# Another order of the gated products: v as a recursive product, gate b as an ordinary one, branch b joined by an adding DMA

## What is computed

```
xn = RMSNorm(x);  u, v, q, k, v_att, g_a, g_b = split(xn @ w_in);  u, v = gelu(u), gelu(v)
a  = u * (tril(W_s[g]) @ RMSNorm(v) + bias)          # chunks of 128 positions, 8 groups
b  = sliding-window attention(q, k, v_att)           # window 128, sinks, distance penalty
h  = sigmoid(g_a) * (a @ w_oa) + sigmoid(g_b) * (b @ w_ob)
x  = x + h @ w_out
x  = x + relu(RMSNorm(x) @ w_up)^2 @ w_down;  y = RMSNorm(x)
```

## Time and profile before

| | us |
|---|---|
| median of 3 runs | 1648.48 |
| lowest and highest | 1646.39, 1648.78 |
| the profiled execution | 1646.17 |
| its span in the trace | 1644.4 |
| mean granted TensorE clock in it | 0.975 of full |

### The profile page before, as it was taken

How to read it: one execution, slowest core, us unless ns; L and a number is a source line. 1 busy time by engine, 2 the same in 40 slices (tenths; PEclk the granted TensorE clock), 3 DMA queues, 4 the chain that set the end, 5 groups by cost and what they waited for, 6 DMA issues and landing times.

```text
span 1644.4 us, 28816 instructions
## 1 busy us (share of the span) xinstructions
PE 1558.3 (95%) x12226; PEld 1522.2 (93%) x12226; DVE 1063.0 (65%) x1385; ACT 764.7 (47%) x1158; POOL 171.1 (10%) x198
## 2 busy tenths in 40 slices
PE   3999999999998999989995999999999999999998
PEld 3988888889997999989995999999999999999997
DVE  3455554402656687666775776786787668767875
ACT  5465555522643555545441474533553355335533
POOL 4222322200001000000000040000000000000001
PEclk7899999999998999999997999999999999999999
DMA  7610110132974465665547444636363636454522
GB/s 243 194 28 25 31 29 21 34 90 78 230 255 133 103 167 155 193 180 162 134 141 233 127 104 103 164 94 179 81 177 92 165 105 153 115 142 127 131 64 104
DMA packets 108649, 209.09 MB, mean 127 GB/s; under 512 B 16816, under 2 KB 44464, under 8 KB 101192
## 3 DMA queue, kind: packets, MB, share of 16 engines
q1 hardware_dynamic: 93760, 140.32, 25.4%
q0 software_dynamic: 8208, 59.77, 18.5%
q10 hardware_dynamic: 6552, 7.13, 1.3%
HBM read 125.99 MB, written 23.53 MB: 91 GB/s over the span
## 4 chain that ended last, share of the span: by engine, by line
PE 80%; DMA 6%; DVE 5%; ACT 4%; issue 2%; SPq 1%; POOL 1%; DVEq 0%; ACTq 0%; POOLq 0%
PE ps L1537 63%; PE ps L1330 10%; PE ps L1318 2%; DMA og<-o_keep 1%; ACT prob L746 1%; DMA og<-h_keep 1%; PE ps L1376 1%; DVE prob L1008 1%; PE ps L1394 1%; DMA raw<-in_w_in 1%; POOL prob L580 1%; PE ps L1515 1%; DMA xn<-xn_keep 1%; SPq L407 1%; DVE y_t L1307 1%
## 5 line engine op out<-in xcount | busy, mean ns | idle before, releaser
L1537 PE MATMUL ps<-xp_hi,wp_hi 128*128 128x258 f32 x3136 | 635.6, 284 | 26.7 <-DVE xp_lo L1118 18.0
L1537 PE MATMUL ps<-xp_lo,wp_hi 128*128 128x258 f32 x3136 | 636.4, 284 | 0.0
L1537 PE MATMUL ps<-xp_hi,wp_lo 128*128 128x258 f32 x3136 | 635.2, 284 | 0.0
L1537 PEld LDWEIGHTS ps<-xp_hi,wp_hi 128*128 128x128 f32 x3136 | 491.1, 191 | 28.3 <-DVE xp_lo L1118 18.5
L1537 PEld LDWEIGHTS ps<-xp_hi,wp_lo 128*128 128x128 f32 x3136 | 490.7, 191 | 0.0
L1537 PEld LDWEIGHTS ps<-xp_lo,wp_hi 128*128 128x128 f32 x3136 | 487.6, 190 | 0.0
L682 ACT ACTIVATE wp_hi<-wbuf 128x1024 fp32r<-128x1024 f32 x196 | 208.0, 1061 | 569.3 <-PE ps L1537 563.7
L1112 DVE TENSOR_TENSOR wp_lo<-wbuf,wp_hi 128x1024 fp32r<-128x1024 f32 x196 | 243.5, 1242 | 163.7 <-ACT wp_hi L682 163.6
L1330 PE MATMUL ps<-xn_hi,w_hi 128*128 128x344 f32 x480 | 160.5, 334 | 2.5 <-DVE q_st L988 2.5
L1330 PE MATMUL ps<-xn_hi,w_lo 128*128 128x344 f32 x480 | 155.9, 325 | 0.0
L1330 PE MATMUL ps<-xn_lo,w_hi 128*128 128x344 f32 x480 | 155.9, 325 | 0.0
(11 more groups left out here) (188 smaller groups left out, 1559.8 us busy)
## 6 DMA issues: line engine op xcount, KB each, us to landing
wbuf<-wbuf POOLq DMA_DIRECT2D x57, 1024.0 KB, 7.6
wbuf<-in_w_up SPq DMA_DIRECT2D x24, 1024.0 KB, 5.5
wbuf<-in_w_down SPq DMA_DIRECT2D x24, 1024.0 KB, 5.1
wbuf<-in_w_in SPq DMA_DIRECT2D x18, 1024.0 KB, 6.6
raw<-in_w_in SPq DMA_DIRECT2D x40, 256.0 KB, 3.4
wbuf<-in_w_ob SPq DMA_DIRECT2D x6, 1024.0 KB, 8.6
wbuf<-in_w_oa SPq DMA_DIRECT2D x6, 1024.0 KB, 5.0
wbuf<-in_w_out SPq DMA_DIRECT2D x6, 1024.0 KB, 5.5
```

The lines of the kernel that those rows point to most:

```text
L1537: last = mm(ps[:, 2 * p + b, 0:HN], w[:, (2 * n + p // 2) % 2, k, p % 2 * P:(p % 2 + 1) * P], x[n % 2][:, k, b * HN:(b + 1) * HN], start=( ...
```

## The change

The order of groups becomes w_ob, v, u, gate a, w_oa, w_out: v is now group 1 (`G_V`), computed in seven block products with gelu on ACT half by half, and the v stage stands between `G_V` and `G_U`. The eight ordinary jobs of stage 1 now compute g_b; ACT copies it to `gate_b` (the place of `mix`) and takes the sigmoid at w = 0 to 7 of group 0. `finish_ob` on DVE multiplies each half of b @ w_ob by its half of `gate_b` and SP stores it to `h_keep`, once. In group G_OA, `finish_oa` only multiplies by gate a; the half of `h_keep` is added by a DMA that POOL issues (`add_h`). `og` and `o_keep` are gone. `xn` is reloaded in four quarters, from w = 12 of group 0 on, with no v stage behind it, and the load of s2 comes ahead of the results' stores at w = 12 (and ahead of `res` in G_OA). `gv_row` and `bb` are loaded at w = 10 of G_V. The first weight quarters of w_ob are loaded in another order and earlier, the buffers swap places, and `sgu_raw` moves.

```diff
-        G_OB, G_U, G_GB, G_GA, G_OA, G_OUT, G_UP = range(7)
+        G_OB, G_V, G_U, G_GA, G_OA, G_OUT, G_UP = range(7)
-        late = [G_OB, G_U, G_OUT, G_UP] + down
-        by_act = [G_U, G_GB, G_GA, G_OUT] + up
-        by_dve = [G_U, G_GB, G_OA] + up
+        late = [G_OB, G_V, G_U, G_OUT, G_UP] + down
+        by_act = [G_V, G_U, G_GA, G_OUT] + up
+        by_dve = [G_OB, G_U, G_OA] + up
...
-            def load_og(g, m):
-                src = o_keep if g == G_GB else h_keep
-                sp.dma_start(og[:, :, :], keep_half(src, m)).then_inc(og_in, 16)
...
+            sp.wait_ge(pv_done, NU)
+            load_quarter(0, "12")
             sp.wait_ge(db_ready, 1)
-            load_quarter(0, "12")
+            load_quarter(0, "11")
             sp.wait_ge(w_split, JW + 2)
             load_quarter(0, "s2")
-            sp.wait_ge(wt_turned, 1)
+            sp.wait_ge(job_done, JW + 1)
             load_quarter(0, "21")
-            sp.wait_ge(job_done, JW + 1)
-            load_quarter(0, "11")
             load_quarter(0, "22")
             for g in range(NM):
                 for w in range(14):
...
+                    if g == G_OB and w == 12:
+                        sp.wait_ge(xp_split, 2 * 7)
+                        for kh, th in ((1, 0), (0, 0), (0, 1), (1, 1)):
+                            cols = slice(th * HT, (th + 1) * HT)
+                            sp.dma_start(xn[:, MH * kh:MH * kh + MH, cols],
+                                         xn_keep[MH * P * kh:MH * P * (kh + 1), cols].rearrange("(k p) t -> p k t", p=P)).then_inc(xn_in[kh, th], 16)
+                    if w == 12 and g + 1 < NM:
+                        sp.wait_ge(wp_split, 14 * (g + 1))
+                        load_quarter(g + 1, "s2")
                     for e, m in finished(g, w):
-                        keep_and_fetch(e, m)
...
+                        if e == G_OB:
+                            sp.wait_ge(*dve_done(e, m))
+                            sp.dma_start(keep_half(h_keep, m), c_half(gate, m)).then_inc(h_kept[m // 2], 16)
...
+            def add_h(m):
+                pool.wait_ge(h_kept[m // 2], 2 * 16)
+                pool.wait_ge(*dve_done(G_OA, m))
+                pool.dma_start(c_half(h_t, m), keep_half(h_keep, m), accum_op=ALU.add).then_inc(h_added[m], 16)
...
-            add_s3(1)
+            add_s3(G_V)
+            add_s2(G_V)
+            add_s4(G_V)
+            add_s1(G_V)
+            add_s3(G_U)
             for t in range(NTOK):
...
                 add_s1(g)
+                if g == G_OA:
+                    for m in range(4):
+                        add_h(m)
+                    add_s3(G_OUT)
+                    for m in range(4, 8):
+                        add_h(m)
...
-                    elif g == G_U:
-                        act.wait_ge(xn_in[int(i != 1)], 16)
+                    elif g == G_V:
+                        act.wait_ge(xn_in[int(i != 1), int(i == 6)], 16)
...
                     elif g == G_OUT:
-                        act.wait_ge(*dve_done(G_OA, m))
+                        act.wait_ge(h_added[m], 16)
...
-                if g == G_OB and w == 13:
+                if g == G_V and w == 13:
                     for t in range(NTOK):
                         r, bank = ROWS[t], 2 * (t % 2)
+                        if t == 2:
+                            finish(G_V, 7)
...
+            def finish_ob(m):
+
+                mh, n = C_ORDER[m // 2][0], m % 2
+                dve.wait_ge(*c_moved(G_OB, m))
+                dve.wait_ge(gate_ready, MH * mh + 2 * n + 2)
                 c = c_half(gate, m)
-                tt(c, c, og[:, :, :], ALU.mult).then_inc(fin_v, 1)
+                tt(c, c, c_half(gate_b, m), ALU.mult).then_inc(fin_v, 1)
...
-                chain.link(tt(c, c, c_half(gate, m), ALU.mult))
-                dve.wait_ge(og_in, 16 * (8 + m + 1))
-                tt(c, c, og[:, :, :], ALU.add).then_inc(fin_v, 1)
+                tt(c, c, c_half(gate, m), ALU.mult).then_inc(fin_v, 1)
...
+                elif g == G_V:
+                    dve.wait_ge(xn_in[0, 0], 16)
+                    dve.wait_ge(xn_in[0, 1], 16)
...
                 elif g == G_OUT:
-                    dve.wait_ge(*dve_done(G_OA, 6 + n))
+                    dve.wait_ge(h_added[6 + n], 16)
...
             def turn_v(t):
                 r, bank = ROWS[t], 2 * (t % 2)
-                pe.wait_ge(*(moved(G_OB, 6, t) if t < 2 else (vn_ready, t - 1)))
+                pe.wait_ge(*act_done(G_V, 3 if t < 4 else 7))
+                pe.wait_ge(*(moved(G_V, 6, t) if t < 2 else (vn_ready, t - 1)))
```

More of the change, by code:

```diff
@@ L36, in build_trunk @@
                 sinks, w_oa, w_ob, w_out, ln2_g, w_up, w_down, lnf_g,
-                y_prompt, y_sample, k_win_p, v_win_p, k_win_s, v_win_s, sgu_v_s, x_keep, xn_keep, o_keep, h_keep):
+                y_prompt, y_sample, k_win_p, v_win_p, k_win_s, v_win_s, sgu_v_s, x_keep, xn_keep, h_keep):
     P = 128
@@ L144, in build_trunk @@
         xg = place("xg", [P, 3, KT, P], F32, r_2 + 4 * D)
+        gate_b = place("gate_b", [P, KT, T], F32, r_2)
         mix = place("mix", [P, KT, T], F32, r_2)
@@ L292, in build_trunk @@
         adds_up = [G_OUT] + down
[L293 to L295 removed]
+        late = [G_OB, G_V, G_U, G_OUT, G_UP] + down
+        by_act = [G_V, G_U, G_GA, G_OUT] + up
+        by_dve = [G_OB, G_U, G_OA] + up
         x_of = [b_all, xn, xn, xn, mix, h_t] + [xf, r_f] * NC
[L297 to L298 removed]
+        c_of = [gate, mix, gate, gate, h_t, res] + [r_f, res] * NC
+        w_of = [(w_ob, 0, 0), (w_in, 0, OV), (w_in, 0, OU), (w_in, 0, OGA), (w_oa, 0, 0), (w_out, 0, 0)]
         for c in range(NC):
@@ L497, in _ @@
                         load_quarter(g + 1, "22")
-                    if g == G_OB and w == 10:
-                        sp.wait_ge(xp_split, 2 * 6)
+                    if g == G_V and w == 10:
+                        sp.wait_ge(xp_split, 2 * (7 * G_V + 6))
                         sp.dma_start(gv_row[:, :], sgu_norm_g.to_broadcast([P, D])).then_inc(gain_in, 16)
@@ L652, in _ @@
                                         ALU.pow).then_inc(v_rstd, 1)
-            for g in range(1, NM):
-                if g not in (G_U, G_UP):
+            for g in range(G_U, NM):
+                if g not in (G_U, G_OUT, G_UP):
                     add_s3(g)
@@ L862, in out_act @@
                     m = 2 * C_ORDER.index(OUT_AT[i]) + p // 2
-                    if g == G_U and i == 0:
-                        act.wait_ge(o_kept, 8 * 16)
-                    elif g == G_GB:
+                    if g == G_V:
+                        act.wait_ge(*dve_done(G_OB, m))
+                    elif g == G_U:
+                        act.wait_ge(h_kept[m // 2], 2 * 16)
+                    elif g == G_GA:
                         act.wait_ge(*dve_done(G_U, m))
-                    elif g == G_GA:
-                        act.wait_ge(h_kept[m // 2], 2 * 16)
                     act.wait_ge(prod_done, 28 * g + 4 * i + p + 1)
@@ L877, in finish @@
                     nc.scalar.activation(c, c, ACT.Square).then_inc(fin_a, 1)
-                elif g in (G_U, G_GB, G_GA):
+                elif g in (G_V, G_U, G_GA):
                     act.wait_ge(*c_moved(g, m))
-                    nc.scalar.activation(c, c, ACT.Gelu_apprx_tanh if g == G_U else ACT.Sigmoid).then_inc(fin_a, 1)
+                    nc.scalar.activation(c, c, ACT.Sigmoid if g == G_GA else ACT.Gelu_apprx_tanh).then_inc(fin_a, 1)
                 elif g == G_OUT:
@@ L923, in _ @@
                 for e, m in finished(g, w):
-                    finish(e, m)
+                    if (e, m) != (G_V, 7):
+                        finish(e, m)
                 if g == G_OB and w < KT:
@@ L1187, in x_sum2 @@
                 b = blocks(g, n)
-                if g == G_U:
+                if g == G_V:
+                    dve.wait_ge(xn_in[1, 1], 16)
+                elif g == G_U:
                     dve.wait_ge(vs_stored, 16)
                     dve.wait_ge(mixed, NTOK)
-                    dve.wait_ge(xn_in[1], 16)
                 dve.wait_ge(t_added, t_count(g, 1 + n))
@@ L1271, in _ @@
                         finish_oa(m)
+                    elif e == G_OB:
+                        finish_ob(m)
                 if g == G_OB and w >= 12:
@@ L1288, in _ @@
                     variances(6).then_inc(var_ready, 1)
-                if (g, w) == (G_OB, 13):
+                if (g, w) == (G_V, 13):
                     out_dve(h)
@@ L1511, in mix_v @@
                 pe.wait_ge(vn_ready, t + 1)
-                pe.wait_ge(*(moved(G_OB, 6, 2 + t) if t < 2 else (mix_ready, t - 1)))
+                pe.wait_ge(*(moved(G_V, 6, 2 + t) if t < 2 else (mix_ready, t - 1)))
                 for g in range(GS):
@@ L1560, in _ @@
                     product(n // 7, n % 7, p)
-                    if n == 6 and p == 2:
-                        pe.wait_ge(v_ready, KT)
+                    if n == 7 * G_V + 6 and p == 2:
                         turn_v(0)
```

(4 more changed lines are left out.)

60 lines of the change are left out of this document (14 added, 46 removed).

## The result

The changed kernel took 1637.49 us as the median of 4 runs (1636.33 to 1638.29) beside 1648.18 of the kernel before (1646.39 to 1648.78): a ratio of 0.9945, interval 0.9923 to 0.9966. It is faster, by 10.7 us between the medians and by 9.1 (5.6 to 12.7) by the ratio, which is not the plain ratio of the two medians (0.9935). The forecast was 1629, in a range of 1615 to 1639: the direction and the range held, the size did not; 19.5 us of gain were forecast, and 8.8 of them (10.4 by the ratio) did not come. The profiled execution took 1637.21 us, its span 1635.5.

A forecast was written before the change was run, and what follows sets the result against it. PE, busy 1558.3 of 1644.4 us, was taken as the bound, with gain only from its stops or slow stretches. 1646.2 - 9.9 - 19.8 - 2.5 + 5.3 + 9.1 = 1628.4, plus 0.6: forecast 1629, range 1615 to 1639.

The forecast's parts named there:

- What goes: Stage 2: both waits for `og` and their stops are removed, 9.9 us and 19.8 us with the restarts.
- The v stage: Between G_V and G_U: shorter first stop and less slowed mixing, -2.5 us, bounds 0 and -3.5.
- First place, G_OB to G_V: PE waits before G_V behind the first quarter of `xn`, starting near T+3.3: +5.3 us with restart, at most +9.
- T: The end of G_OB, 494.8 us in the trace of the kernel before.
- Second place, G_OA to G_OUT: PE waits at G_OUT's second block product behind `res`: +7.1 us, +9.1 with restart, bounds 0 to +15.
- count three of the four: G_OA to G_OUT: three adding DMAs of h halves 4 to 7 run ahead of `res`, 2.7 us each, 8.1 us.
- T': When G_OUT's first matmuls ran, 866.1 us in the trace of the kernel before.
- POOL would get more than half: At G_OUT: POOL's larger packets put all four adds ahead of `res`, sum 2.7 us longer; kept apart from the sum.
- (b): Rival: both new stops, at G_V and G_OUT, are longer; 1636 to 1643 us; chance 0.16.
- (a): Rival: the new stops hardly come, since SP's queue is served ahead of POOL's; 1614 to 1620 us; chance 0.24.
- (c): Rival: slower through the adding DMA into `h_t`, eating the other gains from 11.3 us a half on; chance 0.04.
- (d): Rival: `og` waits go, but weights were the last thing at both stops; 1643 to 1649 us; chance 0.04.

The follow-up runs named there:

- e3: The changed kernel with POOL's add of s2 for G_OUT issued only when both halves of `res` have landed: 1632.9 us, ratio 0.9922.
- e2: The changed kernel with POOL's add of s3 for G_OUT ahead of the add of half 2 instead of behind half 3: 1627.7 us, ratio 0.9891.
- e4: The changed kernel without the eight adding DMAs of `h_keep` into `h_t`, so branch b is left out of h: 1620.9 us, ratio 0.9860.
- e7: The changed kernel with POOL's eight DMAs of `h_keep` as plain copies that overwrite `h_t`, without the addition: 1630.5 us, ratio 0.9910.
- e8: The kernel before with only `finish_oa` and `add_h` as in the change, gate b and its `og` as before: 1639.7 us, ratio 0.9973.
- e11: The changed kernel with the load of s2 in G_OA put back behind the two loads of `res`: 1630.4 us, ratio 0.9905.
- e5: The changed kernel with POOL's add of s3 for G_V held back until the first quarter of `xn` has landed: 1635.6 us, ratio 0.9937.
- e12: The changed kernel with weight quarter 22 of G_V loaded behind `xn` and s2 instead of ahead of them: 1633.8 us, ratio 0.9931.
- e13: The changed kernel with `res` in quarters, the first ahead of s2, s3's add early, quarter 22 behind s2, G_OUT's sums for halves 6 and 7 later: 1615.7 us, ratio 0.9821.

## Why the prediction was right or wrong

**What goes**: right. No `og`, and no stop between G_U and G_OA.

**The v stage**: right in kind, too small. From the end of the last block product to G_U's first matmul it took 35.1 us (494.8 to 529.9); now, with the last product's end at 581.2 less one turning of 0.9, it takes 580.3 to 610.5, 30.2 us: -4.9 against -2.5, and past the bound of -3.5. The first stop is 1.1 us where 1.3 were forecast, and the mixing behind it is not slowed:

```profile
581.84 1.29 DVE vn L1242
...
583.17 2.05 PE ps L1516 x16
```

The first stop gave 2.0 us. Of the difference of 3.52 and 2.05 half was counted, and all of it came, 1.5. The last mixing, which the sum left out, took 1.9 us for 3.0, another 1.1.

**First place, G_OB to G_V**: right. The quarter of `xn` landed at 493.97 = T+1.5 (T now 492.4) where T+0.8 was forecast. The stop was 4.1 us for 3.3. The restart cost more than 2.0 us, by the windows behind the two stops, beside the earlier trace rows (first the length and the busy time of PE with its count of matmuls, here 75, then the other engines; the last three numbers are the mean granted clock, the DMA share and GB/s):

```profile
885.62:897.20 11.58, 11.58 (x75) 11.58 (x76) 11.17 (x12) 3.08 (x3) 0.18 (x1) 0.75 0.62 160
496.53:508.10 11.57, 11.57 (x75) 11.57 (x76) 7.99 (x8) 4.43 (x6) 0.85 (x1) 0.75 1.05 387
```

75 matmuls instead of 98 are 2.7 us for each stop. The mean granted clock of 0.75 is a stretch at 1.2 GHz within one at 2.4, after PE had stood for 4 us as after it had stood for 19.

**Second place, G_OA to G_OUT**: the step that failed is the count of work ahead of `res`: "count three of the four". The place, the transfer that PE would wait for and, within 0.4 us a half, the prices were right; the term of 8.1 us for POOL's work was mis-sized. POOL's queue took 23.2 us before `res` was in. Two things were left out. The add of s3 had been moved behind `add_h` of half 3, so it ran from about T'-8 to T'-3 ahead of SP's load of s2; the sum has no term for it. And the two queues were read as one line, first come, first served, so that half 7 and the add of s2, issued some 12 us and more after `res`, were taken to come behind it. Half 7 landed at 876.5, 6.6 us before `res`, and e3 shows that the add of s2 came before its end too. e2 takes the first away and with it most of the second: `res` landed at T'+16.1 and the stop was 7.0 us, where T'+16.3 and 7.1 stand in the prediction. An agreement so close is in part luck: in e2 POOL's work ahead of `res` was 11.5 us, not 8.1, and SP's own was 14.4 (59.0% of the same 24.4 us), not 15.7. The bound of +15 named the right cause (all four halves and the add of s2) but not s3. It was 4 us short of the stop of 18.7.

The prediction's sentence that POOL would get more than half, since its packets are larger, does not fit here for the halves. Between 860 and 874 the packets of q0 were about 2 KB and those of q1 about 4 KB, 704 and 706 of them, and each queue had 54% of the engines. It fits the add of s2: between 876 and 880 POOL's queue moved 88 packets of 8 KB and had 84% of the engines, beside 74 of SP's with 19%.

**The sum.** 1628.4 + 1.5 (G_V: 4.1 + 2.7 for 5.3) + 12.3 (G_OUT: 18.7 + 2.7 for 9.1) - 2.4 (v stage) = 1639.8; the first group of stage 2 also began at 411.12 instead of 412.86, 1.7 less, which can't be told from noise (the end of group 0 lies between 492.3 and 495.6 in runs whose code up to there is the same). That makes 1638.1 for 1637.2 measured in the profiled execution.

**The rivals.** (b), both stops longer, is what happened at one of the two places, and the measured time lies in its 1636 to 1643. (a) fell: SP was not served ahead of POOL; the two took turns, and up to 850 POOL had the engines alone. (c) fell by e4 and e7: 3.0 us a half, far from 11.3. (d) fell.

**What was not forecast** is how the gain divides. The adding DMA alone is worth 4.4 us (e8, 1.5 to 7.6), and s2 ahead of `res` costs about 7 (e11). With that order undone the change is at 0.9905, and e8, with the same order, at 0.9973. So all the rest of the change, gate b's new place and the earlier v above all, brings the larger part, about 11 us together. No run takes these apart.

## What to carry to other kernels

When a stop goes, list every transfer that is issued between the last idle moment of the DMA engines and the next need, in both queues, and ask of each add or load that was moved in a queue what stands in front of it now: a transfer off the critical path (s3, needed some 35 us into the group) was the dearest one here. A large load that one early user waits for should be cut and waited for piece by piece (18.7 us of stop became 5.4), and loads with late needs (22, s2) go behind those with early ones.

## What the runs showed of the hardware

- Two DMA queues with work share the 16 engines, whichever was issued first. Between 860 and 882 they moved 911 and 896 packets, so the share goes by what a packet costs. The second of the two loads of `res` (2.1 MB each, on SP's queue) landed 35.2 us after its issue beside POOL's adds in the changed kernel, 18.5 in the kernel before, and 20.6 beside the add of s2 and the start of that of s4 (e4).
- A DMA that adds costs twice a plain one of the same size and shape: 3.0 to 3.1 us of all engines for 516 KB against 1.4. It was also moved in more packets, 272 against 144 a half (10384, 9360 and 8208 packets of q0 in the change, e7 and e4). The adds of 1 MB from buffer to buffer cost 5.3 us each; a 1 MB load from HBM, another route, cost 3.1.
- The restart after a stop of 3.4 us (e4) cost 15 of 98 matmuls, 1.8 us, at a mean granted clock of 0.85:

```profile
870.29:881.87 11.58, 11.58 (x83) 11.58 (x84) 11.58 (x13) 3.08 (x3) 0.38 (x1) 0.85 0.39 113
```

  Shorter stops divide in two. Behind the stop of 1.9 us in e5 (and the same behind 2.0 us in e12) 15 matmuls are missing as well, 1.8 us:

```profile
519.78:531.36 11.58, 11.58 (x83) 11.58 (x84) 9.02 (x9) 7.96 (x9) 0.85 (x1) 0.85 0.81 163
```

  Behind those of 1.1, 0.8 and 1.4 us in e13 it is 2 of 98 each, and the granted clock stays at 1.00:

```profile
495.54:507.12 11.58, 11.58 (x96) 11.58 (x97) 10.50 (x11) 4.55 (x6) 0.84 (x1) 1.00 1.05 397
519.74:531.32 11.58, 11.58 (x96) 11.58 (x97) 10.46 (x10) 7.96 (x9) 0.85 (x1) 1.00 0.81 166
879.08:890.66 11.58, 11.58 (x96) 11.58 (x97) 11.58 (x13) 6.14 (x8) 0.85 (x1) 1.00 0.84 172
```

  So a stop of 1.9 us cost 3.7 in all here, more than half of what the stop of 4.1 before G_V had cost with its restart (6.8), and e5 gained little. Stops of one length in other surroundings were not tried.
